# Order of the steps inside two attention stages and one projection stage of a hybrid backbone

## The reference

```python
q = rms_norm((h @ wq).reshape(B, S, 2 * DA_HEADS, DA_HEAD_DIM), qn)
k = rms_norm((h @ wk).reshape(B, S, 2 * DA_HEADS, DA_HEAD_DIM), kn)
v = (h @ wv).reshape(B, S, DA_HEADS, DA_V_DIM)
q, k = rope_2d(q, row, col), rope_2d(k, row, col)      # latent tokens only
s = jnp.einsum('bqhd,bkhd->bhqk', qblk, k) * scale
p = jax.nn.softmax(s, axis=-1)
w = p[:, :, 0] - lam * p[:, :, 1]                      # the two halves of a head
o = jnp.einsum('bhqk,bkhd->bqhd', w, v)
```

## Time and profile before

| | us |
|---|---|
| median of 3 runs | 4579.6 (4575.07 to 4581.31) |
| the profiled execution | 4575.91 |
| its span | 4574.1 |
| PE, DVE, ACT, POOL busy | 4032.6, 3321.3, 1685.3, 783.8 |

### The profile page before, as it was taken

How to read it: one execution, slowest core, us unless ns; L and a number is a source line. 1 busy time by engine, 2 the same in 40 slices (tenths; PEclk the granted TensorE clock), 3 DMA queues, 4 the chain that set the end, 5 groups by cost and what they waited for, 6 DMA issues and landing times. The chain is left out here.

```text
span 4574.1 us, 55467 instructions
## 1 busy us (share of the span) xinstructions
PE 4032.6 (88%) x20840; PEld 3356.2 (73%) x20840; DVE 3321.3 (73%) x6710; ACT 1685.3 (37%) x2864; POOL 783.8 (17%) x532
## 2 busy tenths in 40 slices
PE   6998888997799999999978687689357999999998
PEld 5544556997699999999843554559357999999997
DVE  2704641798799999999823313317997999999998
ACT  1110431106644444444423333311075444444443
POOL 0000000000133333333200000000002333333332
PEclk8996889987999999999987887899689999999999
DMA  4410002224899999999720010020048999999997
GB/s 187 171 54 11 1 19 106 75 93 146 296 420 416 410 405 404 406 402 407 317 101 20 1 37 1 1 96 11 1 137 331 420 415 404 405 406 402 407 403 287
DMA packets 234651, 1032.92 MB, mean 226 GB/s; under 512 B 15920, under 2 KB 117232, under 8 KB 126320
## 3 DMA queue, kind: packets, MB, share of 16 engines
q0 software_dynamic: 76032, 553.68, 30.1%
q1 hardware_dynamic: 158352, 475.70, 26.7%
HBM read 969.92 MB, written 59.39 MB: 225 GB/s over the span
## 5 line engine op out<-in xcount | busy, mean ns | idle before, releaser
L1267 POOL DMA_INDIRECT xT<-in_uv,rows x172 | 257.1, 1495 | 2662.8 <-POOLq L913 2218.8
L1267 POOL DMA_INDIRECT gbuf<-in_uv,rows x340 | 517.8, 1523 | 873.8 <-DVE hT L1434 804.0
L1434 DVE SCALAR_TENSOR_TENSOR hT<-gbuf,act,hT 128x1024 f32<-128x1024 f32 x336 | 416.9, 1282 | 6.0
L1419 DVE SCALAR_TENSOR_TENSOR gbuf<-gbuf,ht 128x1024 f32<-128x1024 f32 x340 | 402.1, 1220 | 2.8 <-DMA gbuf<-in_uv,rows 2.8
L99 PE MATMUL ps<-hT,ring 128*128 128x512 f32 (+1 forms) x624 | 334.9, 620 | 47.7 <-DMA ring<-in_wts 32.2
L1281 PE MATMUL ps<-h1h,U1h 128*128 128x384 f32 x1024 | 344.8, 337 | 9.8 <-DVE U1l L1393 9.8
L1281 PE MATMUL ps<-h0h,U0h 128*128 128x384 f32 x1024 | 344.3, 336 | 9.5 <-DVE U0l L1393 9.5
L1281 PE MATMUL ps<-h1h,U1l 128*128 128x384 f32 x1024 | 344.6, 337 | 0.0
L1281 PE MATMUL ps<-h1l,U1h 128*128 128x384 f32 x1024 | 344.3, 336 | 0.0
L1281 PE MATMUL ps<-h0h,U0l 128*128 128x384 f32 x1024 | 344.0, 336 | 0.0
L1281 PE MATMUL ps<-h0l,U0h 128*128 128x384 f32 x1024 | 343.6, 336 | 0.0
(11 more groups left out here) (334 smaller groups left out, 9260.5 us busy)
## 6 DMA issues: line engine op xcount, KB each, us to landing
ring<-in_u SPq DMA_DIRECT2D x128, 1024.0 KB, 12.9
ring<-in_v SPq DMA_DIRECT2D x128, 1024.0 KB, 9.3
ring<-in_wts SPq DMA_DIRECT2D x26, 2048.0 KB, 8.2
gates<-ring SPq DMA_DIRECT2D x24, 2048.0 KB, 9.0
ring<-gates SPq DMA_DIRECT2D x64, 768.0 KB, 16.2
xT<-in_ada_late SPq DMA_DIRECT2D x24, 1024.0 KB, 4.8
abuf<-in_ada_mid POOLq DMA_DIRECT2D x16, 1024.0 KB, 5.2
gbuf<-in_uv,rows POOLq DMA_INDIRECT x340, 10.6
```

Of the source, the lines that this page charges most:

```text
L1267: pool.indirect_dma_start(out=slots[m % GSLOTS], out_offset=None, in_=inp[f"uv{l}"], in_offset=bass.IndirectOffsetOnAxis(ap=rows[:, c:c + ...
L1419: v.scalar_tensor_tensor(u, u, 1.0, ht[:, m // P, :], ALU.mult, ALU.mult, accum_out=act4[:, n % 2, m % 2:m % 2 + 1]).then_inc(sem(n_ + "do ...
L1434: v.scalar_tensor_tensor(y, x, w, y, ALU.mult, ALU.add).then_inc(sem(n_ + "acc"), 1)
```

## The change

In `diff_qkv` the rotation product of a column now stands on TensorE two products behind it, with one round of column sums for each product; VectorE rotates behind the round of weighing. The root of q is no longer multiplied into q: it is transposed (`turn_sd`) and kept in `rsq`, which the attention block uses as the scale of its exponentials. The root of k is spread between the value products. `diff_attention` gets a third buffer in `pr`; values and transposes are one item later and change places; VectorE runs ahead by one item. `mla_attention` changes the places of values and transposes too, and there VectorE no longer runs ahead. The wait for the two stores moves from the projection block into the attention block. The rest of the diff (one set of semaphores for both expert layers' row transfers, `rsq` made at the top) changes names and places alone.

```diff
     def diff_qkv(ring, indT, qT, kT, V, rsq, cos, sin, scr, abuf):
+                def rotate(i):
+                    if i:
+                        pe.wait_ge(sem("rot_v"), 3 * (i - 1) + 1)
+                    product(pe, bank2(6), rot_da, (qT, kT)[i // 8][:, i % 8, 0:T], True, True).then_inc(sem("rot_mm"), 1)
+                def turn_sd():
+                    pe.wait_ge(sem("sd_a"), 2)
+                    for tb in range(TB):
+                        mm = pe.transpose(ps[:, 5, 256 + tb * 16:256 + (tb + 1) * 16], sd_q[:, tb * P:(tb + 1) * P],
+                                          ident[0:16, 0:16])
+                    mm.then_inc(sem("sd_t"), 1)
+                def spread_k(nb):
+                    if nb == 0:
+                        pe.wait_ge(sem("rs_v"), 2)
+                    else:
+                        pe.wait_ge(sem("k_v"), nb)
+                    product(pe, bank2(4), indT[:, 0, nb, :], sd_k, True, True).then_inc(sem("k_mm"), 1)
                     if i >= 1:
                         squares(i - 1)
-                    if 1 <= i <= N_MID // 2:
-                        for m in (2 * i - 2, 2 * i - 1):
-                            column_sums(m, 1 + 2 * ((i + 1) % 2))
+                        column_sums(i - 1)
+                    if i >= 2:
+                        rotate(i - 2)
                 squares(15)
+                column_sums(15)
+                rotate(14)
+                values(0)
+                rotate(15)
+                values(1)
+                turn_sd()
+                for i in range(2, 10):
+                    values(i)
+                    spread_k(i - 2)
...
+                for m in range(N_MID):
+                    weigh(m)
+                    if m == 1:
+                        v.wait_ge(sem("da_in"), 64)
+                    if m >= 2:
+                        rotated(m - 2)
+                rotated(14)
+                rotated(15)
...
     def diff_attention(qT, kT, V, rsq, oT, pr, pT):
+            @block.sync
+            def _(sp):
+                sp.wait_ge(sem("stored"), 32)
...
-                for w in range(len(items) + 2):
+                for w in range(len(items) + 3):
                     if w < len(items):
                         scores(w)
-                    if 1 <= w <= len(items):
-                        turns(w - 1)
-                    if w >= 2:
-                        values(w - 2)
+                    if w >= 3:
+                        values(w - 3)
+                    if 2 <= w < len(items) + 2:
+                        turns(w - 2)
...
+                maxima(0)
+                for w in range(M):
+                    if w + 1 < M:
+                        maxima(w + 1)
+                    weights(w)
...
-                                       scale=scale, accum_out=z[:, 4 + c:5 + c]).then_inc(sem("da_exp"), 1)
+                                       scale=rsq[:, 2, qb, 2 * hd + c:2 * hd + c + 1], accum_out=z[:, 4 + c:5 + c]).then_inc(sem("da_exp"), 1)
...
     (mla_attention)
                     if w < len(items):
                         scores(w)
+                    if w >= 2:
+                        values(w - 2)
                     if 1 <= w <= len(items):
                         turns(w - 1)
-                    if w >= 2:
-                        values(w - 2)
...
-                maxima(0)
                 for w in range(len(items)):
-                    if w + 1 < len(items):
-                        maxima(w + 1)
+                    maxima(w)
                     weights(w)
```

More of the change, by code:

```diff
@@ new lines, in rotate, with values @@
+                def rotate(i):
+                    if i:
+                        pe.wait_ge(sem("rot_v"), 3 * (i - 1) + 1)
+                    product(pe, bank2(6), rot_da, (qT, kT)[i // 8][:, i % 8, 0:T], True, True).then_inc(sem("rot_mm"), 1)
+                def values(i):
+                    c, tb = divmod(i, 5)
+                    if tb == 0:
+                        chunk_in(pe, J_WV + c)
+                    if i == 2:
+                        pe.wait_ge(sem("rot_v"), 3 * 15 + 1)
+                    if i >= 4:
+                        pe.wait_ge(sem("v_copied"), i - 3)
+                    w = ring[:, (J_WV + c) % SLOTS, :].rearrange("p (c n) -> p c n", c=DC)
+                    for dc in range(DC):
+                        mm = pe.matmul(ps[:, V_BANKS[i % 4], :], hT[:, dc, tb * P:(tb + 1) * P], w[:, dc, :],
+                                       start=dc == 0, stop=dc == DC - 1)
+                    mm.then_inc(sem("v_mm"), 1)
@@ L337, in _, with weigh @@
             def _(v):
-                s = sem("ad_acc")
-                for m in range(N_MID):
+                def weigh(m):
+                    s = sem("ad_acc")
                     w = abuf[:, m % 2, :].rearrange("p (c n) -> p c n", c=DC)
@@ L440, in _, with z_, at, maxima @@
                 s = sem("da_w")
-                for w, (hd, qb) in enumerate(items):
-                    n, k0 = width(qb), 8 * w
-                    z = small[:, 16 * (w % 2):16 * (w % 2) + 16]
+                M = len(items)
+                def z_(w):
+                    return small[:, 16 * (w % 2):16 * (w % 2) + 16]
+                def at(w, k):
+                    if k <= 4:
+                        return k if w == 0 else 8 * w - 4 + k
+                    return 8 * w + k + (4 if w + 1 < M else 0)
+                def maxima(w):
+                    hd, qb = items[w]
+                    n, z = width(qb), z_(w)
                     for c in range(2):
@@ L482, in results @@
                     act.copy(oT[:, hd, qb * P:(qb + 1) * P], ps[:, 6 + w % 2, 0:P]).then_inc(sem("da_o"), 1)
-                for w in range(len(items) + 2):
+                for w in range(len(items) + 3):
                     if w < len(items):
                         exps(w)
-                    if 1 <= w <= len(items):
-                        copies(w - 1)
-                    if w >= 2:
-                        results(w - 2)
+                    if 2 <= w < len(items) + 2:
+                        copies(w - 2)
+                    if w >= 3:
+                        results(w - 3)
     def diff_subnorm(indT, oT, scr):
```

156 lines of the change are left out of this document (68 added, 88 removed).

## The result

The changed kernel takes 4336.0 us (median of 4 runs, 4334.4 to 4338.9), against 4580.5 us (4575.1 to 4584.8) for the kernel before on the same chip. The ratio is 0.9471, with a 95% interval of 0.946 to 0.9483: faster by 244 us. The profiled execution took 4336.2 us, with a span of 4334.4.

The account below looks back on a forecast made before the run. Bounds: TensorE in the projection's first two parts, TensorE and VectorE alternating in its tail, engine-to-engine chains in attention. 63 + 28 + 130 = 221; 4575.9 - 221 = 4355, about 4357 with the median's distance; range 4320 to 4400.

Parts of the forecast that it names:

- three terms: Predicted gains: projection minus 63 us, differential attention minus 28, both latent attention stages together minus 130.
- The steps: Projection loop: each step takes 12.2 us on TensorE, from 10.03 + 0.91 + 1.27.
- a dip of the clock: Projection: 2 us of the gain given back for a slower clock somewhere.
- The slack of VectorE: Projection loop: VectorE's 8.5 us a step is hidden behind TensorE with 3.7 us to spare.
- VectorE as the bound (4380): Projection rival: rotation late by 1.5 us a step, 24 us more; chance 0.10 shared with another latent attention wait.
- late transfers as a loss: Projection rival: late modulation columns stall every second TensorE step, costing from 16 us landing; slower or no change 0.02.
- The two chains: Latent attention: VectorE and ScalarE in series, 2.95 us an item, and a chain over two items, 3.0 an item.
- the old chain: Latent attention before: maximum, weights, transposes, value product and next score in series, 4.78 us for a full item.
- the 1.78 us in which TensorE waited: Latent attention before: from maximum start to transposes, while VectorE ends maximum and weights; the value product would stand there.
- TensorE waits for `pT` before the value products: Sign that the prediction is wrong: TensorE waiting for the transposed weights before value products; no size given.
- the chain over two items: Latent attention: maximum to exponential, exponential, copy, value product, transposes, next score and handovers, 6.0 us for two items.
- The rival built on the old clock (4390): Attention stages and projection: the clock swings as before, the gain is only 185 us; chance 0.20.

Follow-up runs that it names:

- the run with the projection alone: The changed kernel with both attention blocks' orders put back to those before, the differential scale still read from the tile: 4522.1 us, ratio 0.9874.

## Why the prediction was right

The forecast of 4357 was 21 us above the time, within its range, and each of its three terms was too small: 63 of 67, 28 of 33, 130 of 142. Of these 21 us some 2 were lost again in stages that weren't touched, so that 221 stands against 239.7 between the two profiled executions. The forecast's own sum, 4354.9 and 3.7, is 4358.6 rather than 4357. All three errors have the same sign, and most of them come from allowances that weren't needed.

**Projection.** The steps held: 12.0 us for 12.2, the last operation on k ends at 384.75 for 386.6, the attention starts 1.3 us later. The term gives back 2 us for a dip of the clock that hardly came (0.99 and 1.00). The slack of VectorE (3.52 for 3.7) and that of the transfers were read rightly, and the latter was tested: with a round's lead taken away, VectorE waits 3.5 us a step and nothing else moves. By this, VectorE as the bound (4380) and late transfers as a loss fall. How the 67 us divide among the moved rotations, the root of q that is no longer multiplied in and the moved wait for the stores was tested by no run.

**Differential attention.** Items of 3.61 and 3.31 us, for 3.65 and 3.3. The stage came out at 151.3 for 156, of which 6 were for the clock. The clock was low only at the entry, where the first two items took 4.68 and 4.67 us, about 2 us too long together. The cost of reading the scale was put at almost nothing, and so it is, but only under the new order: in the serial one it is 0.21 us in each full item. That the third buffer is what makes the look-ahead pay was not in the prediction at all; with two buffers the same look-ahead loses 46 us against the old order with the same scales. The sum counted VectorE's work and TensorE's work, and took for granted that neither holds the other up across items. With three buffers that was so; it was right by the kernel's design, not by the argument.

**Latent attention.** The items are 2.84 to 2.98 us for 2.9 to 3.0, and the stages take 121.5 and 121.7 us for 127. Eight heads take 115.8 us for 118, and fill, drain and slow clock together 5.7 for 9. The two chains that the prediction set up for the new order were right, above all that of VectorE and ScalarE in series. Its reason why the old chain goes, which it gives first, is not the one that carries the gain. The prediction says that the value product now stands in the 1.78 us in which TensorE waited. That holds with the look-ahead kept, and gives 2.22%; with the look-ahead gone there is nothing left to fill, and its removal alone gives 3.00 of 3.11%. The value product's new place, on top of that, is worth at most the 0.11% between the two, which is less than the intervals. The prediction names both edits in one sentence and never prices them apart.

The text says it would be wrong if TensorE waits for `pT` before the value products. It does, by 0.79 us, and the forecast stands: the copy and its place in the chain over two items were in the sum (6.0 us for two). As a test the sentence was badly chosen; as a sign it was good, since this wait marks what could still be gained.

**The clock.** In the stages where TensorE's gaps shrank, the granted clock rose from 0.88, 0.83 and 0.82 to 0.95, 0.96 and 0.96, and to 0.76 it fell where gaps of up to 3.4 us came in (two buffers). What is missing to 1.00 lies at the entry of each stage, in its first 12 to 18 us; this is the changed kernel behind that, in the differential attention and in the first latent group:

```profile
404.00:537.30 133.30, 125.06 (x741) 88.55 (x740) 113.93 (x294) 88.53 (x225) 0.00 (x0) 1.00 0.00 1
2417.00:2526.40 109.40, 94.10 (x611) 74.31 (x609) 56.16 (x148) 60.46 (x151) 0.00 (x0) 1.00 0.00 1
```

Gaps remain in both: 17 of up to 0.79 us in the latent window, and in the other such as this one:

```profile
417.68 1.61 PE L441 MATMUL ps<-kT,qT 64*128 64x512 f32 x3 [0.39 <-ACT pr_da L527]
```

The Trainium skill (page "TensorE: Matmul & The Clock Gate", section "A second HAM failure mode: psum-queue depth-cycling") tells of one bf16 kernel whose TensorE idled briefly between groups of matmuls so often that its clock swung. Taken as a rule for any such kernel, as the prediction takes it, this would have left the clock of before; the trace after doesn't agree, at 1.00 with the gaps just named. The rival built on the old clock (4390) falls with it.

What stays open: the gain between the medians is 244 us and between the two spans 240, a difference within the spread of the kernel before (9.7 us); and the cause of the 2 us lost in the last expert stage isn't known. Nor is it shown why the clock of the differential attention was 0.83 in the run with the projection alone, with nearly the gaps of before, and what the third buffer would give there without look-ahead.

## What to carry to other kernels

Look-ahead on an in-order engine is a debt: the work put first may wait for an engine that waits for the work put second. Before writing "next item's maximum, then this item's weights", ask whether the score of the next item stands behind this item's transposes; if it does, take another buffer and delay the transposes by an item, or drop the look-ahead. With the buffer there, try on every engine the operation that is ready first, and the one that others wait for, ahead of the long one. In the latent attention that was the copy ahead of the exponential and the transposes ahead of the product, and it was worth 36 us; in the differential one, where VectorE is the bound, the places on TensorE were worth nothing. Price the clock apart for the entry of a stage and for what follows: here the first 12 to 18 us were slow, and the rest was at 1.00 with gaps of up to 0.79 us left.

## What the runs showed of the hardware

An activation of 128x640 takes 0.88 us with its scale read from a tile and 0.79 with a constant scale; on a serial chain that became, with two scaled products of 0.21 for 0.15 us, 0.21 us an item. Under cover almost nothing of it is left: 3.61 us for an item, where 4.54 less the wait of 0.95 makes 3.59. What the low clock cost depended on the item: in the kernel before, short items of the differential attention took 3.33 us at a clock of 1.00 and 4.94 at 0.65, and full ones 4.54 at 1.00 and up to 4.93 at 0.65. The granted clock of that attention stage was 0.95 in the changed kernel, 0.88 in the kernel before, 0.83 in the run with the projection alone, and 0.76 with two buffers.
